# Differential attention: means per token, scores from rounded halves, and the combination of the two softmaxes on POOL

## The reference

```python
        q = rms_norm(q, q_norm_g[l])           # 4 heads, 2 halves of 64 columns each
        k = rms_norm(k, k_norm_g[l])
        lam = (exp(sum(lambda_q1 * lambda_k1)) - exp(sum(lambda_q2 * lambda_k2)) + lam_init)
    # diff_attention, per block of 128 queries:
        s = jnp.einsum("bqhcd,bkhcd->bhcqk", qi, k, preferred_element_type=jnp.float32) * scale
        s = jnp.where(mask, s, -jnp.inf)       # causal
        p = jax.nn.softmax(s, axis=-1)
        a = (p[:, :, 0] - lam * p[:, :, 1]).astype(v.dtype)
        return jnp.einsum("bhqk,bkhe->bqhe", a, v)
    o = rms_norm(o, subln_g) * (1.0 - lam_init)
    # and around it
        merged = (gates[:, :, 0] * jnp.matmul(conv_out, w_conv_out[l])
                  + gates[:, :, 1] * jnp.matmul(attn_out, w_attn_out[l]))
        x = x + jnp.matmul(merged, w_out[l])
        h2 = rms_norm(x, ffn_norm_g[l])
        x = x + hierarchical_moe(h2, ...)
```

## Time and profile before

| | us |
|---|---|
| median of 3 runs | 3426.29 (3418.71 to 3426.93) |
| the profiled execution | 3406.21 |
| its span | 3404.4 |
| busy in the span: PE, DVE, ACT, POOL | 2888.0, 2039.9, 1440.5, 490.3 |
| differential attention, norms | 2014 to 2091 |
| differential attention, loop | 2091 to 2226 |
| mean granted TensorE clock | 0.926 of 2.4 GHz |

### The profile page before, as it was taken

How to read it: one execution, slowest core, us unless ns; L and a number is a source line. 1 busy time by engine, 2 the same in 40 slices (tenths; PEclk the granted TensorE clock), 3 DMA queues, 4 the chain that set the end, 5 groups by cost and what they waited for, 6 DMA issues and landing times. The chain is left out here.

```text
span 3404.4 us, 36710 instructions
## 1 busy us (share of the span) xinstructions
PE 2888.0 (85%) x13228; PEld 2306.9 (68%) x13236; DVE 2039.9 (60%) x2225; ACT 1440.5 (42%) x2102; POOL 490.3 (14%) x407
## 2 busy tenths in 40 slices
PE   6976886999997997999949975967899669999991
PEld 5865565888885765787737853655687658888881
DVE  4773645334443554344453889878345679999993
ACT  3341333333333665343333342333332257777770
POOL 0001310000002666000000000000000024334430
PEclk9986898999997999999979997989899879999996
DMA  3100010112445663111111100010111569999995
GB/s 87 50 13 4 0 37 25 48 45 99 148 160 124 140 140 81 56 50 44 44 62 56 50 21 0 1 31 19 50 50 44 187 227 393 375 377 374 371 340 230
DMA packets 221418, 396.27 MB, mean 116 GB/s; under 512 B 73316, under 2 KB 73444, under 8 KB 221283
## 3 DMA queue, kind: packets, MB, share of 16 engines
q1 hardware_dynamic: 212064, 377.66, 33.6%
q0 software_dynamic: 9216, 16.80, 1.3%
HBM read 356.32 MB, written 54.85 MB: 121 GB/s over the span
## 5 line engine op out<-in xcount | busy, mean ns | idle before, releaser
L2258 DVE TENSOR_TENSOR ex_w<-ex_raw,ex_w 128x2048 fp32r<-128x2048 f32 x192 | 437.1, 2290 | 51.3 <-ACT ex_w L2205 49.8
L2205 ACT ACTIVATE ex_w<-ex_raw 128x2048 fp32r<-128x2048 f32 x192 | 365.4, 1916 | 113.9 <-DMA ex_raw<-in_w_down_e 41.4
L2135 PE MATMUL ps<-ex_w,ex_xT 128*128 128x512 f32 x1536 | 366.9, 395 | 6.3 <-DVE ex_xT L2267 6.2
L2135 PEld LDWEIGHTS ps<-ex_w,ex_xT 128*128 128x128 f32 x1536 | 286.3, 189 | 70.7 <-DVE ex_xT L2267 6.4
L756 DVE TENSOR_TENSOR bs_t<-arena,bs_t 128x1024 fp32r<-128x1024 f32 x80 | 98.0, 1225 | 259.6 <-ACT bs_t L720 259.6
L613 DVE SCALAR_TENSOR_TENSOR arena<-arena,small 128x1023 f32<-128x1023 f32 (+9 forms) x168 | 213.7, 1272 | 4.3
L720 ACT ACTIVATE bs_t<-arena 128x1024 fp32r<-128x1024 f32 x80 | 84.9, 1061 | 298.2 <-PE ps L699 270.9
L697 PE MATMUL ps<-bs_t,bs_w 128*128 128x512 f32 x512 | 201.1, 393 | 11.2 <-DVE bs_w L759 9.1
L1059 POOL TENSOR_TENSOR fa_pl<-fa_p,fa_ph 128x512 fp32r<-128x512 f32 x192 | 191.7, 1012 | 100.3 <-ACT fa_ph L1176 97.6
L756 DVE TENSOR_TENSOR za_t<-arena,za_t 128x1024 fp32r<-128x1024 f32 x64 | 78.4, 1226 | 208.8 <-ACT za_t L720 208.7
L698 PE MATMUL ps<-bs_t,bs_w 128*128 128x512 f32 x512 | 200.3, 391 | 0.0
(11 more groups left out here) (372 smaller groups left out, 6959.3 us busy)
## 6 DMA issues: line engine op xcount, KB each, us to landing
ex_raw<-in_w_gate_e SPq DMA_DIRECT2D x64, 1024.0 KB, 13.5
ex_raw<-in_w_up_e SPq DMA_DIRECT2D x64, 1024.0 KB, 13.5
ex_raw<-in_w_down_e SPq DMA_DIRECT2D x64, 1024.0 KB, 13.7
arena<-in_w_in SPq DMA_DIRECT2D x108, 512.0 KB, 3.5
arena<-in_x SPq DMA_DIRECT2D x4, 2048.0 KB, 11.3
arena<-in_w_out SPq DMA_DIRECT2D x16, 512.0 KB, 3.7
arena<-expert_out SPq DMA_DIRECT2D x8, 1024.0 KB, 12.9
arena<-in_w_branch_ssm SPq DMA_DIRECT2D x8, 512.0 KB, 3.6
```

Source lines behind the costliest of these rows:

```text
L2135: mm = nc.tensor.matmul(out, l, r, start=(k == 0 and n == 0), stop=(k == kc - 1 and n == 2))
L2205: nc.scalar.activation(half_of(part[m][0], h), raw[m][:, h * W // 2: (h + 1) * W // 2], ACT.Identity).then_inc(high[m], 1)
L2258: V.tensor_tensor(half_of(part[m][1], h), raw[m][:, h * W // 2: (h + 1) * W // 2], half_of(as_f32(part[m][0]), h), ALU.subtract)\
```

## The change

**Norms.** The mean of a tile is now taken per token: for each of eight blocks of 128 tokens the squares are the stationary operand and two columns of the matrix of 1/64 the moving one, so the result has tokens on partitions and two columns (one per half). Keys come first. The root and reciprocal are taken of 64 columns once for all keys (`rk`), once for all queries (`rq`). The keys' reciprocals are transposed to rows, split into a rounded high part and the rest, and spread over the partitions by a matmul with a selecting matrix (`pick`); DVE scales the key by gain and by the spread value. Queries are not scaled: their reciprocal enters the exponential as ACT's scale per partition, and the bias becomes maximum x reciprocal, a further DVE instruction per score, awaited by ACT. Both gains go to the keys. Queries and keys are split into high and low parts. ACT's list has squares 6 and 7 ahead of the keys' high parts.

**Loop.** A score is three fp32r products over the 64 partitions of its half. The combination is done by POOL in two instructions; the copies of the transposes and the store move to ACT; DVE keeps the maxima, the bias and the small reciprocals, in a new order.

**Residual.** The work tiles move to region 4, so x1 is written to memory under "n2", and read back in "b2" behind weight load 4.

```diff
 def phase_dense(..., fetch=None, fetched=None):
                 sp.dma_start(raw[u % 2], jobs[j][1][:, k:k + 2, :]).then_inc(wload[u % 2], 16)
...
+                if u == 4 and fetch is not None:
+                    fetch(sp)
...
                     elif kind == "add":
+                        dve.wait_ge(fetched, 16)
...
         @block.gpsimd
-            for h in range(DH):
-                for r in range(2):
-                    nc.gpsimd.memset(q_of[h][r][(1 - r) * DHD:(2 - r) * DHD, :], 0.0)\
-                        .then_inc(filled, 1)
+            for n in range(NU):
+                s = n % 2
+                w = (UNITS[n][1] + 1) * P
+                pool.wait_ge(exped, 2 * n + 2)
+                pool.wait_ge(weighed, 2 * n + 2)
+                first_, second = prob[s][0][:, 0:w], prob[s][1][:, 0:w]
+                nc.gpsimd.tensor_scalar(second, second, coef[n % 3], None, ALU.mult)\
+                    .then_inc(multiplied, 1)
+                pool.wait_ge(multiplied, n + 1)
+                nc.gpsimd.tensor_tensor(first_, first_, second, ALU.add).then_inc(combined, 1)
...
         @block.tensor
+            def mean(n):
+                x = ORDER[n]
+                pe.wait_ge(squared, n + 1)
+                for t in range(TT):
+                    at = t * NH + 2 * (x % DH)
+                    mm = nc.tensor.matmul(c.ps[:, int(x < DH), at:at + 2], sq[n % 2][:, t * P:(t + 1) * P],
+                                          halves_of[:, 0:P:DHD], start=True, stop=True)
+                mm.then_inc(meaned, 1)
...
             def score(m):
                 h, t = UNITS[m // 2]
+                r = m % 2
...
                 if m >= 2:
                     pe.wait_ge(exped, m - 1)
+                q = [x[half(r), t * P:(t + 1) * P] for x in q_of[h]]
                 for b in range((n + BANK - 1) // BANK):
                     width = min(BANK, n - b * BANK)
-                    nc.tensor.matmul(c.ps[:, S_BANK[m % 2] + b, 0:width],
-                                     q_of[h][m % 2][:, t * P:(t + 1) * P],
-                                     k_of[h][:, b * BANK:b * BANK + width],
-                                     start=True, stop=False, skip_group_check=True)
+                    diag = (b + 1) * BANK >= n
+                    k = [x[half(r), b * BANK:b * BANK + width] for x in k_of[h]]
+                    to = c.ps[:, S_BANK[r] + b, 0:width]
+                    nc.tensor.matmul(to, q[0], k[0], start=True, stop=False, skip_group_check=True)
+                    nc.tensor.matmul(to, q[0], k[1], start=False, stop=False, skip_group_check=True)
+                    nc.tensor.matmul(to, q[1], k[0], start=False, stop=not diag, skip_group_check=True)
...
-            pe.wait_ge(filled, 4 + 2 * DH)
-            pe.wait_ge(normed, 3 * DH)
-            pe.wait_ge(rooted, NN)
+            pe.wait_ge(filled, 4)
+            for n in range(DH):
+                mean(n)
+            turn_rows()
+            mean(DH)
+            mean(DH + 1)
+            spread_rows(0)
+            spread_rows(1)
+            mean(DH + 2)
+            spread_rows(2)
+            mean(DH + 3)
+            spread_rows(3)
...
         @block.scalar
+            square(DH)
+            high_q(3)
+            square(DH + 1)
...
+            square(DH + 2)
+            square(DH + 3)
+            high_k(0)
+            high_k(1)
...
+            for n in range(NU):
...
+                for r in range(2):
+                    act.wait_ge(shifted, 2 * n + r + 1)
+                    if n >= 2:
+                        act.wait_ge(turned, first[n - 1])
+                    at = t * NH + 2 * h + r
+                    nc.scalar.activation(prob[n % 2][r][:, 0:w], flat(S_BANK[r])[:, 0:w], ACT.Exp,
+                                         scale=rq[:, at:at + 1], bias=bias[:, r:r + 1],
+                                         accum_out=rowsum[n % 3][:, r:r + 1]).then_inc(exped, 1)
+                if n:
+                    take_T(n - 1)
                 if n >= 2:
+                    store(n - 2)
...
         @block.vector
                 V.tensor_reduce(negmax[:, r:r + 1], flat(S_BANK[r])[:, 0:w], AX.X, ALU.max,
                                 negate=True).then_inc(negated, 1)
+                dve.wait_ge(negated, m + 1)
+                V.tensor_tensor(bias[:, r:r + 1], negmax[:, r:r + 1], rq[:, at:at + 1], ALU.mult)\
+                    .then_inc(shifted, 1)
+
+            def invert(n):
+                z = n % 3
                 dve.wait_ge(exped, 2 * n + 2)
-                if n >= 2:
-                    dve.wait_ge(stored, n - 1)
-                V.reciprocal(rinv[s], rowsum[s]).then_inc(weighed, 1)
+                if n >= 3:
+                    dve.wait_ge(stored, n - 2)
+                V.reciprocal(rinv[z], rowsum[z]).then_inc(weighed, 1)
                 dve.wait_ge(weighed, 2 * n + 1)
...
-                dve.wait_ge(weighed, 2 * n + 2)
-                V.scalar_tensor_tensor(out=prob[s][0][:, 0:w], in0=prob[s][1][:, 0:w],
-                                       scalar=coef[s], in1=prob[s][0][:, 0:w], op0=ALU.mult,
-                                       op1=ALU.add).then_inc(combined, 1)
...
             maxima(0)
             maxima(1)
-            for n in range(NU + 1):
-                if n < NU:
-                    combine(n)
-                for m in (2 * n + 2, 2 * n + 3):
-                    if m < 2 * NU:
-                        maxima(m)
-                if n < NU:
-                    take_T(n)
-                if n:
-                    store(n - 1)
+            for n in range(NU):
+                if n + 1 < NU:
+                    maxima(2 * n + 2)
+                invert(n)
+                if n + 1 < NU:
+                    maxima(2 * n + 3)
...
+        def keep_x1(sp):
+            sp.dma_start(x1_dram.rearrange("(t p) d -> p t d", p=P),
+                         R(4).rearrange("p (t d) -> p t d", t=TT)).then_inc(x1_kept, 16)
+            sp.wait_ge(x1_kept, 16)
```

More of the change, by code:

```diff
@@ L1445, in phase_diff_attention @@
     S_BANK = (4, 6)
-    NN = 2 * DH
+    ORDER = [DH + h for h in range(DH)] + list(range(DH))
+    half = lambda r: slice(r * DHD, (r + 1) * DHD)
     with ExitStack() as ctx:
@@ L1572, in _ @@
                 if n >= 2:
[L1573 to L1576 removed]
+                    store(n - 2)
+            take_T(NU - 1)
+            store(NU - 2)
+            store(NU - 1)
         @block.vector
```

233 lines of the change are left out of this document (141 added, 92 removed).

## The result

The changed kernel takes 3549.75 us (median of 4 runs, 3545.55 to 3554.65), the kernel before beside it 3426.61; the ratio is 1.0363, with a 95% interval of 1.034 to 1.0386. The direction and the mechanism were as predicted. The size was not: the change costs 123 us where I had 44.5, and 3549.75 lies outside 3438 to 3520.

What follows compares the result with a forecast made beforehand. DVE was taken as the bound, PE close behind. Norms -37.6, ring +66.1 and clock +16 gave +44.5 us on the median of 3426.3, so 3470.8 us, range 3438 to 3520.

Steps and rivals of the forecast that it cites:

- the ring: Loop: invert, POOL, turn, values, score, maximum go round once per unit without overlap; 197.9 us against 131.8, +66.1.
- The norms: Norms of queries and keys: first maximum starts at 2053.9 instead of 2091.5, -37.6 us, bounds -30 to -50.
- The squares: Norms, ACT's list: last two squares ahead of high_k cost nothing; behind it they would delay the last means some 3 us.
- The residual: x1 written out before the stage and read back in the last dense stage: costs nothing.
- The small pieces of DVE: Loop, 32 units: one maximum of two 23.6 us, bias product 6.4, invert 14.4, hand-overs between engines 12.8.
- POOL's product: Loop: POOL's multiplication by a column, priced by the one-input affine_select, 21.8 us, upper bound 37.8.
- The sum: Loop: POOL's addition in the combination, 37.8 us, upper bound 45.2.
- the clock in the loop: Loop: a fifth of PE's 20.3 us a head doubles at 1.2 GHz, +16 us, bounds 0 and 40.
- PE's piece at the full clock: Loop, 32 units: turn 15.8 us, values 33.7, one score of two 31.6.
- The dear ring: Rival: POOL at two-input prices (+90), half of PE's part slow (+40), norms -30; +100, 3526 us; chance 0.13.
- The cheap ring: Rival: clock up throughout, norms at -50, POOL at its lower bound (59); +9, 3436 us; chance 0.14.
- the other side: Rival: the ring doesn't close, POOL finishing during PE's second score; norms' gain stands, about 3380 us; chance 0.07.

Runs made afterwards that it cites:

- e1: Changed kernel with invert(n) moved ahead of maxima(2n+2) in DVE's list, nothing else: 3461.74 us, ratio 1.0113.
- e11: Changed kernel with e4's unused matmuls and e5's form of POOL's product together: 3488.12 us.
- e6: Changed kernel with the squares of the keys' first two tiles put back behind their high parts on ACT: 3554.9 us.
- e5: Changed kernel with POOL's product as a tensor_tensor, the coefficient's column spread over the row, instead of a tensor_scalar: 3530.88 us.
- e4: Changed kernel with 2(t+1) matmuls of 512 columns, results unused, ahead of each PE wait for POOL's combination: 3514.16 us.
- e2: Changed kernel with the combination as one DVE instruction at invert's place, behind maxima(2n+2), instead of on POOL: 3452.57 us.
- e9: e1 with the exponential's bias made by a one-input DVE tensor_scalar instead of a two-input tensor_tensor: 3466.56 us.
- e10: e9 plus e5's form of POOL's product and a coefficient made by a one-input tensor_scalar: 3462.65 us, ratio 1.0078.
- e12: e10 with t+1 matmuls, results unused, ahead of each wait for the combination: 3426.76 us, ratio 0.9988.
- e8: Changed kernel with e2's DVE combination, e1's order, and unused matmuls after each mean and ahead of the scores: 3415.54 us, ratio 0.9968.

## Why the prediction was right and wrong

**Right.** *The direction and the ring.* The step that I called my choice, that invert(n+1) stands behind maxima(2n+4) and closes a ring through POOL, turn, values and score, is shown three ways: by the circle of waits, by e1 (-85.4 us for moving that one step), and by e11, where the terms add up to 0.5 us. *The norms.* -32.6 us against -37.6, within -30 to -50. *The squares.* 3.9 us against some 3 (e6). *The residual and the time behind the stage.* Nothing lost there. *The small pieces of DVE.* Maximum 24.0 against 22.1 (both for 30 turns); the hand-overs, bias and coefficient were too dear in my sum rather than too cheap (19.6 against 31.5). *The ends.* Outside the 30 turns lie 18.5 us, where two turns of mean length and the 3 us of an open pipeline make 16.4: 3.5 from the first maximum to the first product, a first turn of 4.5, and 10.5 from the last product to the next stage.

**Wrong: POOL's product, 21.8 us.** It measured 55.2, outside my upper bound of 37.8 as well. The step that failed is the choice of the one-input affine_select as the nearest row: I took the number of inputs for what sets the price, and let the price of a two-input row be the ceiling. e5 shows that on POOL the number of inputs doesn't set it: the one-input tensor_scalar with a column takes 2857 ns for 1024 columns, the tensor_tensor with the same column spread out 1893, the tensor_tensor with two whole tiles 2338. The line was weak in itself too, since its row at 512 columns is bfloat16 and the one at 128 float32. The sum was mis-sized by less, 44.7 against 37.8, inside its bound of 45.2 (L1059's slope comes to 45.7, when I work it out again); I had drawn its line through L508, whose second operand is a spread-out small one, where L1059's slope with two whole operands was the better row. Together 40 us.

**Wrong: the clock in the loop, a fifth of PE's share, +16.** It measured 42 (e4), just past my bound of 40, and it wasn't a fifth at the low level but most of it: a mean of 0.63 between 0.50 and 1.00 is three quarters of the time at 0.50, and the 0.57 of PE's own stretches is six sevenths. The row I took it from, the state-space stage with PE's records covering 66 of 80 us at 0.91, is a much busier stretch; here they cover 196 of 295. I saw that the pauses were longer and still took a small value from it. A dearer POOL also makes longer pauses, but the error in the product did little to the clock: 18 us less of it left the clock at 0.63 (e5), and the two savings add up (e11). With all of POOL's steps gone the closed ring still had 0.74 (e2). What the pauses alone do to the clock was not separated from what else is in the loop.

**Wrong by less: PE's piece at the full clock.** I had 76.0 us for 30 turns; 94.4 remain at a loop clock of 0.93 (e4) and 91.1 at 0.95 (e11), and the estimate above puts it at 87 at the full clock, some 11 too little in my sum. Which of turn, values and score it is I did not separate. The terms have small slips of their own: eight transposes in 0.85 us make 15.3 us for 144, not 15.8, and 27 products of 0.235 us a head make 6.35, not 6.7. They go the other way and come to some 2 us.

**Right in kind, somewhat short: the norms.** The first four means as one line in order of time:

```profile
2017.26 12.81 PE L1508 MATMUL ps<-small,arena 128*128 128x2 f32 x64 [2.50 <-POOL small L1479]
```

12.8 us for four, 3.2 each from the first on, where I had 10.4 (the first at the full clock, the second half so), which is 2.4 of the 5 us. The start at 2017.3 in place of 2016.4 is no part of it: the whole stage starts 0.9 us later in this execution. The other 2.6 us I did not place.

**The rivals.** The dear ring (3526) was the nearest, and its two conditions both came true: POOL at or above two-input prices, and much of PE's part slow. Its price was still too low, since POOL's product had a ceiling that didn't hold. I gave it 0.13, as a joint accident; but much of PE's part being slow was no accident of its own, since it came with the ring whatever the product's price was (e5). The cheap ring fell with the clock and with POOL's price, and the other side with POOL's 3.1 us a unit.

**What I said would show it.** POOL busy some 60 us: 99.9. Turns of 9 to 10 us at the widest tile and 5 at the narrowest: 11.7 at the widest; at the narrowest 4.5 in the first head and 6.9 in the others. PE's longest waits for POOL's sum and DVE's for the mask matmul: both so. A head of 50 to 54 us: 73.8 (a quarter of 295.3). The first maximum 40 us after the start: 44.1. Clock under 0.95: 0.63.

## What to carry to other kernels

Before moving a step to an idle engine, write down each engine's list and look whether the step's input and the release of its output now stand on one closed path: there every piece counts by its full length, and here 100 us of work on an engine that was busy 14% of the time went with a loop 160 us longer. Price an operation by a row of the same engine, the same form of instruction and the same kinds of operands; where there is none, the ceiling is open, and the number of inputs doesn't close it. In a ring of waits TensorE pauses, and filling the pauses here brought its clock from 0.63 to 0.93 and 42 of the 160 us back (e4), so a ring's price can come with a second one on top.

## What the hardware showed unexpectedly

- POOL, 128x1024 float32: tensor_scalar by a column 2857 ns, tensor_tensor with the column spread out 1893, tensor_tensor of two tiles 2338 (after and e5). One full input less was dearer.
- A DVE tensor_tensor of one column of float32, 0.16 us by itself, took until the end of POOL's two-input instruction, 1.26 us in the turn shown and up to 1.6 in e1; a DVE tensor_scalar of the same size took 0.21 us at any moment (e9). Once POOL's product was a tensor_tensor too (e5), the bias was held up under it as well, up to 1.82 us, where under the tensor_scalar of the changed kernel it never was (27 of 27).
- TensorE's clock can eat a saving: in e10 18 us less of POOL came with a clock of 0.65 in place of 0.70 and no time, and filling the pauses gave 36.8 us (e12). And it isn't bought by mere records: in e8 TensorE was busy 49.7 of 52 us at 0.61, and 20.00 of 20 us at 0.50.
- The exponential with a per-partition column as its scale takes 831 ns on average where it was 739, the same shapes:

```profile
L1671 ACT ACTIVATE arena<-ps,small 128x128 f32<-128x128 f32 (+7 forms) x64 | 53.2, 831 | 100.2 <-DVE small L1744 100.2
```

- The router's 128 narrow matmuls took 19.7 us in one execution of the kernel before and 36.6 in another, the rest of the kernel being the same.
